# Thirty transposing loads of the expert activations begun by ScalarE instead of SyncE

## The chip, the cores and the metric

The kernel runs on one core of one Trainium2 chip. The core has five engines, each with an instruction stream of its own: TensorE (PE, matrix products), VectorE (DVE), ScalarE (ACT), GpSimd (POOL) and SyncE (SP, which only begins transfers here). They meet through semaphores: an instruction may wait until a counter has reached a value, and may raise one when it is done. Transfers are begun by SP, ACT or POOL and carried out by 16 shared DMA engines. The metric is the device time of one execution in microseconds; less is better.

## The reference

One decoder block of a first kind is followed by one of a second kind, for 256 tokens of width 2048 in float32. The change lies in the last part of the first block, a layer of 16384 experts of which each token uses 8 x 16:

```python
def peer_ffn(h, w_pq, peer_keys, peer_u, peer_v):
    ...                                   # for each token: idx and gate of 8 heads x 16 experts
    def one_block(args):
        x_blk, i_blk, g_blk = args
        u = jnp.take(peer_u, i_blk, axis=0)
        a = jax.nn.gelu(jnp.einsum("td,thkd->thk", x_blk, u)) * g_blk
        v = jnp.take(peer_v, i_blk, axis=0)
        return jnp.einsum("thk,thkd->td", a, v)
```

The kernel doesn't gather. It multiplies all tokens with all 16384 rows of `peer_u`, applies gelu, multiplies with a dense table of gates that is zero where a token doesn't use an expert, and multiplies the result with all rows of `peer_v`. Beside that it already computes the second block's modulation, `mod = jax.nn.silu(c) @ w_mod[l] + b_mod[l]`, on VectorE.

## The kernel before

**Tiles of weights.** All weights stream through the core as 512 KB tiles (128 partitions x 1024 values). For each tile SP begins a load into one of 8 buffers `raw` (`load`, L445); ACT copies it, rounded, into one of 4 buffers `hi` (`split`, L795 to L802); DVE forms the remainder `lo` = `raw` - `hi` (L1521); PE then runs 12 products of 512 columns on `hi` and `lo` (`tile`, L2657 to L2683). ACT may write the `hi` buffer of tile t+4 when PE has finished tile t, and SP may load tile t+8 when DVE has finished with tile t.

**The expert stage.** The 16384 experts are 32 blocks of 512. A block has 8 tiles of `peer_u` ("up") and 8 of `peer_v` ("down"). After a block's 8 up tiles ACT applies gelu in PSUM and copies the result as 16-bit halves to `Ab` (`gelu`, L1079 to L1088, two instructions of each); POOL stores `Ab` to a scratch in memory (`a_store`, L679). A transposing load brings the scratch back with experts on partitions, into one of two buffers `AT` (`act_in`, L530 to L535; 32 of them). DVE multiplies `AT` with the gates into `P32` (`gate`, L1988 to L1996), ACT rounds that to `Ph` (`act_high`, L1140 to L1144), DVE forms the remainder `Pl` (`low`, L2001), and `Ph` and `Pl` enter the 8 down tiles. The down tiles form four chunks c = 0 to 3 of two tiles each, in two pairs of PSUM banks in turn; when a chunk is complete, DVE adds it to `X` (`v_add`, L2023 to L2029; `pair_add`, L2066 to L2071). PE must not begin chunk 2 before chunk 0 is added, since both use the same banks.

**Order of the blocks.** The up tiles of the first 24 blocks come first (`AHEAD`). Then come 8 main blocks (`MAIN`; L1161 on ACT, L2031 on DVE): 8 up tiles of block 24+v, then 8 down tiles of block v. Their 16 tiles are called tile 0 to 15 here; tile 8 begins the down part, and chunk 0 is tiles 8 and 9, chunk 2 is tiles 12 and 13. Then come 11 pairs of blocks (`act_pair`, L1186, and `dve_pair`, L2073) of 16 down tiles for two blocks in the order of `PAIR`, and a last pair.

**What stands in each queue.** ACT and DVE work through lists written out in the source. In a main block ACT has: splits, with a load of `w_mod` (1 MB, `mod_load`, L1156) after every second one; gelu after the split of tile 11; splits of tiles 12 and 13; `act_high`; further splits. DVE has: splits, with a product of a `w_mod` row (2.28 us, L2020) after every second one; split of tile 12; `gate` of the next block; split of tile 13; `v_add` of chunk 0; `low`; further splits. SP's queue holds the loads of the weights, and `act_in` of the block two further on between the 8 up tiles and the 8 down tiles, or, in a pair, twice between down tiles.

Of the kernel before, what the change touches and what calls it, by code (L numbers as in the profile page):

```python
# [12 lines left out]
U16 = mybir.dt.uint16  # L13
# [7 lines left out]
D, KD = 2048, 16  # L21
# [19 lines left out]
MAIN = NBLK - AHEAD  # L41
# [129 lines left out]
def build(nc, A, out):  # L171
    V, SC, PE_, GP = nc.vector, nc.scalar, nc.tensor, nc.gpsimd
    ctx = ExitStack()
    with ctx:
# [102 lines left out]
        AT = at("AT", [P, 2, JB, S], W0 + 20)  # L277
# [166 lines left out]
        def _(sp):  # L444
# [83 lines left out]
                    load(tile("peer_v", b * (4 * TL) + j), n + j, off)  # L528

            def act_in(v, q):  # L530
                if not isinstance(v, int) or v >= 2:
                    sp.wait_ge(gated, v * 2 - 2)
                sp.wait_ge(a_st, v * 16 + 64)
                block = adram[v] if isinstance(v, int) else adram[bass.ds(v, 1)].rearrange("b s a n -> (b s) a n")
                sp.dma_start_transpose(AT[:, q].bitcast(U16), block.rearrange("s a n -> (s a) n")).then_inc(a_in[q], 16)  # L535

            up(0, n0)
            queries_in(2)
# [6 lines left out]
            with sp.Fori(0, MAIN // 2) as it:  # L545
                for q in range(2):
                    up(it * 2 + (AHEAD + q), n0 + AHEAD * TC + 16 * q, it * 32)
                    act_in(it * 2 + (q + 2), q)
                    down(it * 2 + q, n0 + AHEAD * TC + 16 * q + 8, it * 32)
            with sp.Fori(0, AHEAD // 2 - 1) as b:  # L550
                for i, (e, c) in enumerate(PAIR):
                    if i in (5, 7):
                        act_in(b * 2 + (MAIN + 2 + i // 7), i // 7)
                    for j in range(TL):
                        load(tile("peer_v", b * (8 * TL) + ((MAIN + e) * 4 * TL + c * TL + j)),
                             n0 + AHEAD * TC + 16 * MAIN + TL * i + j, b * 16)
# [235 lines left out]
        def _(act):  # L792
            st = Steps(act, act_step)

            def split(n0, off=0):  # L795
                if n0 >= TOTAL:
                    return
                act.wait_ge(raw_ready[n0 % RAW], 16 * (n0 // RAW + 1) + off * (16 // RAW))
                if n0 >= SPL:
                    act.wait_ge(tile_used, n0 - SPL + 1 + off)  # L800
                w = TW // 2 if n0 in ROPE_TILES else TW
                SC.copy(hi[:, n0 % SPL, 0:w], raw[:, n0 % RAW, 0:w]).then_inc(hi_ready, 1)  # L802
# [276 lines left out]
            def gelu(b, n, bank=0):  # L1079
                act.wait_ge(tile_used, n)  # L1080
                for t in range(TT):
                    SC.activation(ps[:, bank + t], ps[:, bank + t], ACT.Gelu_apprx_tanh,
                                  scale=stat[:, ROOT2 + 2 + t:ROOT2 + 3 + t]).then_inc(scaled, 1)
                if not isinstance(b, int) or b:
                    act.wait_ge(a_st, b * 16 + 48)
                for t in range(TT):
                    act.wait_ge(scaled, b * 2 + (t + 7))
                    SC.copy(Ab[:, t], ps[:, bank + t].bitcast(U16).rearrange("p (n a) -> p a n", a=2)).then_inc(a_ok, 1)  # L1088
# [51 lines left out]
            def act_high(v, q, used):  # L1140
                act.wait_ge(gated, v * 2 + 2)
                if used is not None:
                    act.wait_ge(tile_used, used)
                SC.copy(Ph[:, q], P32[:, q]).then_inc(ph_ok, 1)  # L1144
# [9 lines left out]
            n0 = BASE["peer"] + AHEAD * TC  # L1154

            def mod_load(u, rr):  # L1156
                act.dma_start(mraw[:, u % 4], A["w_mod"][bass.ds(rr * KD + u, 1)].rearrange("a p n -> p (a n)")
                              ).then_inc(mod_in[u % 4], 16)

            act.wait_ge(g_st[1], 32)  # L1160
            with act.Fori(0, MAIN // 4) as rr:  # L1161
                act.wait_ge(mod_used, rr * KD)
                for u in range(2):
                    mod_load(u, rr)
                for i in range(4):
                    n, off = n0 + 16 * i, rr * 64
                    for j in range(4):
                        split(n + 4 + 2 * j, off)
                        split(n + 5 + 2 * j, off)
                        u = 4 * i + j  # L1170
                        if u + 2 < KD:
                            act.wait_ge(mod_used, rr * KD + u)
                            mod_load(u + 2, rr)
                    gelu(rr * 4 + (AHEAD + i), off + (n + 8))
                    split(n + 12, off)
                    split(n + 13, off)
                    act_high(rr * 4 + (i + 1), (i + 1) % 2, off + n)
                    for j in range(14, 20):
                        split(n + j, off)
# [6 lines left out]
            def act_pair(v, n, u):  # L1186

                for p in range(16):
                    if p == 13:
                        act_high(v + 2, 0, n + 14)  # L1190
                    split(n + SPL + p)
                    if p == 0:
                        act_high(v + 1, 1, n)
                    elif p in (4, 6, 10, 12):
                        mod_fetch(u + 2 + (4, 6, 10, 12).index(p))

# [2314 lines left out]
```

## Time and profile before

| | us |
|---|---|
| median of 3 runs (lowest to highest) | 3500.81 (3499.68 to 3501.33) |
| the profiled execution | 3499.71 |
| its span in the profile | 3498.1 |
| PE busy | 3483.0 |
| DVE busy | 2642.4 |
| ACT busy | 1904.9 |

The span runs from the first to the last instruction. An engine is busy while it executes; issuing a transfer doesn't count, but the timeline shows it with a "q" behind the engine's name (ACTq, SPq), and the duration there is the time that the engine's instruction stream spent on the issue. Of the 3498.1 us the main blocks take 1283 to 1631 us, and the pairs 1631 to about 2110 us. A tile takes PE 2.72 us in both. Adjacent instructions of an engine overlap by about 0.1 us in the timeline, so a duration is a little more than the step to the next start.

### The profile page before, as it was taken

The numbers are of one execution on the slowest core, as the hardware profiler recorded it, in microseconds if no ns is written. First come the engines' busy times: TensorE is split into PE (matmuls) and PEld (weight loads), VectorE is DVE, ScalarE is ACT, GpSimd is POOL, SyncE is SP. The second block draws the span as 40 slices with busy tenths as digits, with TensorE's granted clock in tenths as the row PEclk, the third lists the DMA queues.
The fourth block names the chain that finished last, engine by engine and source line by source line (L and its number), as shares of the span: only waits on it lengthen the run. The fifth ranks groups of instructions, "written<-read, shape, count | busy, mean of one in ns | idle before, by whom it ended". The sixth has DMA issues, their size and how long they took to land.

```text
span 3498.1 us, 47372 instructions
## 1 busy us (share of the span) xinstructions
PE 3483.0 (100%) x16532; PEld 2906.2 (83%) x16532; DVE 2642.4 (76%) x3553; ACT 1904.9 (54%) x2469; POOL 150.9 (4%) x207
## 2 busy tenths in 40 slices
PE   9999999999999999999999999999999999999999
PEld 7898888888888888888888888878888888888887
DVE  6654557679888878888888888899976666666668
ACT  6554444555588864444444446557754555545544
POOL 2100000000000000000000001010000000000000
PEclk9999999999999999999999999999999999999999
DMA  8556658876667799999999997655556577877774
GB/s 279 184 159 199 195 175 286 301 231 216 218 217 262 258 321 360 318 334 327 338 338 339 338 338 242 180 178 171 167 176 222 176 222 213 233 230 213 233 228 145
DMA packets 319649, 853.39 MB, mean 244 GB/s; under 512 B 134209, under 2 KB 134849, under 8 KB 305137
## 3 DMA queue, kind: packets, MB, share of 16 engines
q1 hardware_dynamic: 250352, 660.69, 59.6%
q10 hardware_dynamic: 52560, 112.28, 9.3%
q0 software_dynamic: 16560, 78.08, 6.3%
q8 instruction: 110, 1.80, 0.2%
q14 instruction: 67, 0.54, 0.0%
HBM read 773.72 MB, written 49.31 MB: 235 GB/s over the span
## 4 chain that ended last, share of the span: by engine, by line
PE 97%; DVE 1%; ACT 1%; DMA 1%; issue 1%; SPq 0%; POOL 0%; ACTq 0%; DVEq 0%
PE ps L2681 29%; PE ps L2682 29%; PE ps L2683 29%; PE ps L3311 2%; PE ps L2774 1%; PE ps L2775 1%; PE ps L2776 1%; PE ps L3027 1%; PE ps L3315 1%; PE ps L2789 1%; PE ps L3153 0%; DMA mraw<-in_w_mod 0%; PE ps L2724 0%; ACT hi L802 0%; DVE lo L1521 0%
## 5 line engine op out<-in xcount | busy, mean ns | idle before, releaser
L1521 DVE TENSOR_TENSOR lo<-raw,hi 128x1024 fp32r<-128x1024 f32 (+1 forms) x1213 | 1468.2, 1218 | 769.5 <-ACT hi L802 767.8
L802 ACT CAST hi<-raw 128x1024 fp32r<-128x1024 f32 (+1 forms) x1215 | 1270.8, 1048 | 1428.2 <-PE ps L2683 1313.6
L2681 PE MATMUL ps<-hi,xx 128*128 128x512 f32 x2752 | 1083.1, 394 | 1.2 <-DVE lo L1516 0.6
L2682 PE MATMUL ps<-lo,xx 128*128 128x512 f32 x2752 | 1072.2, 390 | 0.0
L2683 PE MATMUL ps<-hi,xx 128*128 128x512 f32 x2752 | 1071.6, 389 | 0.0
L2681 PEld LDWEIGHTS ps<-hi,xx 128*128 128x128 f32 x2752 | 517.0, 188 | 110.9 <-issue 5.5
L2683 PEld LDWEIGHTS ps<-hi,xx 128*128 128x128 f32 x2752 | 516.7, 188 | 109.2
L2682 PEld LDWEIGHTS ps<-lo,xx 128*128 128x128 f32 x2752 | 517.3, 188 | 102.8
L2681 PE MATMUL ps<-hi,Ph 128*128 128x512 f32 x1020 | 397.4, 390 | 0.4 <-DVE X L2029 0.4
L2683 PE MATMUL ps<-hi,Pl 128*128 128x512 f32 x1020 | 396.9, 389 | 0.0
L2682 PE MATMUL ps<-lo,Ph 128*128 128x512 f32 x1020 | 396.8, 389 | 0.0
L2681 PEld LDWEIGHTS ps<-hi,Ph 128*128 128x128 f32 x1020 | 191.4, 188 | 40.4 <-DVE X L2029 0.8
L2683 PEld LDWEIGHTS ps<-hi,Pl 128*128 128x128 f32 x1020 | 191.4, 188 | 39.8
L2682 PEld LDWEIGHTS ps<-lo,Ph 128*128 128x128 f32 x1020 | 191.5, 188 | 39.6
L2681 PE MATMUL ps<-hi,Fh 128*128 128x512 f32 x348 | 135.6, 390 | 0.8 <-DVE Fl L2558 0.7
L2682 PE MATMUL ps<-lo,Fh 128*128 128x512 f32 x348 | 135.4, 389 | 0.0
L2683 PE MATMUL ps<-hi,Fl 128*128 128x512 f32 x348 | 135.4, 389 | 0.0
L2060 DVE SCALAR_TENSOR_TENSOR mraw<-mraw,cS 128x2048 f32<-128x2048 f32 x48 | 109.6, 2283 | 0.0
L1094 ACT ACTIVATE oh<-oh,selR 128x128 fp32r<-128x128 f32 x256 | 82.1, 397 | 13.1 <-DVE oh L1964 13.1
L2537 DVE SCALAR_TENSOR_TENSOR cv<-UP,ccol,cv 128x255 f32<-128x255 f32 (+1 forms) x176 | 73.2, 478 | 8.5 <-ACT cv L1422 7.7
L2681 PEld LDWEIGHTS ps<-hi,Fh 128*128 128x128 f32 x348 | 65.3, 188 | 15.1 <-DVE Fl L2558 1.1
L2020 DVE SCALAR_TENSOR_TENSOR mraw<-mraw,cS 128x2048 f32<-128x2048 f32 x32 | 73.1, 2285 | 5.4 <-DMA mraw<-in_w_mod 5.3
(515 smaller groups left out, 3783.2 us busy)
## 6 DMA issues: line engine op xcount, KB each, us to landing
raw<-in_peer_u SPq DMA_DIRECT2D x256, 512.0 KB, 4.4
raw<-in_peer_v SPq DMA_DIRECT2D x256, 512.0 KB, 6.6
mraw<-in_w_mod ACTq DMA_DIRECT2D x96, 1024.0 KB, 7.8
raw<-in_w_up SPq DMA_DIRECT2D x176, 512.0 KB, 4.2
raw<-in_w_in SPq DMA_DIRECT2D x143, 512.0 KB, 3.6
raw<-in_in SPq DMA_DIRECT2D x128, 512.0 KB, 3.6
raw<-in_w_down SPq DMA_DIRECT2D x88, 512.0 KB, 4.5
raw<-in_out SPq DMA_DIRECT2D x64, 512.0 KB, 4.0
```

The costliest lines, as they stand in the source:

```text
L802: SC.copy(hi[:, n0 % SPL, 0:w], raw[:, n0 % RAW, 0:w]).then_inc(hi_ready, 1)
L1094: low = SC.activation(oh2[:, g % 2, k, 1], oh2[:, g % 2, k, 0].bitcast(F32), ACT.Copy, scale=selR[:, t:t + 1])
L1521: V.tensor_tensor(lo[:, n0 % SPL, 0:w], raw[:, n0 % RAW, 0:w], hi[:, n0 % SPL, 0:w].bitcast(F32), ALU.subtract).then_inc(lo_ready, 1)
L2020: V.scalar_tensor_tensor(mraw[:, u % 4], mraw[:, u % 4], 1.0, cS[:], ALU.mult, ALU.mult, accum_out=mcol[:, bass.ds(rr, 1), u]).then_inc(mo ...
L2060: V.scalar_tensor_tensor(row, row, 1.0, cS[:], ALU.mult, ALU.mult, accum_out=mcol[:, part, u % KD:u % KD + 1]).then_inc(mod_used, 1)
L2537: ins = V.scalar_tensor_tensor(dst, src, ccol[:, q + 1 - tap:q + 2 - tap], dst, ALU.mult, ALU.add)
L2681: PE_.matmul(acc, xhi[:, k0 + k, xs], H, start=s0, stop=False)
L2682: PE_.matmul(acc, xhi[:, k0 + k, xs], L, start=False, stop=False)
L2683: mm = PE_.matmul(acc, xlo[:, k0 + k, xs], H, start=False, stop=s1)
L2774: PE_.matmul(acc, H, xhi[:, k0 + k], start=first and k == 0 and f % 2 == 0, stop=False)
L2775: PE_.matmul(acc, H, xlo[:, k0 + k], start=False, stop=False)
L3311: PE_.matmul(both, H, xx[:, :, k0 + k], start=first and k == 0, stop=False)
```

## The change

Of the 32 transposing loads, SP keeps the first two. The other 30 are taken out of SP's queue and written into ACT's list: in a main block right behind the gelu, ahead of the splits of tiles 12 and 13; in a pair behind the splits of p = 2 and p = 8. They wait for the same two semaphores as before: `gated` (the buffer's last user is done) and `a_st` (the scratch is stored). So that the block number is a constant, ACT's loop over 2 x 4 main blocks is written out.

```diff
             def act_in(v, q):
-                if not isinstance(v, int) or v >= 2:
-                    sp.wait_ge(gated, v * 2 - 2)
                 sp.wait_ge(a_st, v * 16 + 64)
-                block = adram[v] if isinstance(v, int) else adram[bass.ds(v, 1)].rearrange("b s a n -> (b s) a n")
-                sp.dma_start_transpose(AT[:, q].bitcast(U16), block.rearrange("s a n -> (s a) n")).then_inc(a_in[q], 16)
+                sp.dma_start_transpose(AT[:, q].bitcast(U16), adram[v].rearrange("s a n -> (s a) n")).then_inc(a_in[q], 16)
...
                     up(it * 2 + (AHEAD + q), n0 + AHEAD * TC + 16 * q, it * 32)
-                    act_in(it * 2 + (q + 2), q)
                     down(it * 2 + q, n0 + AHEAD * TC + 16 * q + 8, it * 32)
             with sp.Fori(0, AHEAD // 2 - 1) as b:
                 for i, (e, c) in enumerate(PAIR):
-                    if i in (5, 7):
-                        act_in(b * 2 + (MAIN + 2 + i // 7), i // 7)
...
             def mod_load(u, rr):
-                act.dma_start(mraw[:, u % 4], A["w_mod"][bass.ds(rr * KD + u, 1)].rearrange("a p n -> p (a n)")
-                              ).then_inc(mod_in[u % 4], 16)
+                act.dma_start(mraw[:, u % 4], A["w_mod"][rr * KD + u]).then_inc(mod_in[u % 4], 16)
+
+            def act_in(v, q):
+                act.wait_ge(gated, v * 2 - 2)
+                act.wait_ge(a_st, v * 16 + 64)
+                act.dma_start_transpose(AT[:, q].bitcast(U16), adram[v].rearrange("s a n -> (s a) n")).then_inc(a_in[q], 16)
 
             act.wait_ge(g_st[1], 32)
-            with act.Fori(0, MAIN // 4) as rr:
+            for rr in range(MAIN // 4):
                 act.wait_ge(mod_used, rr * KD)
                 for u in range(2):
                     mod_load(u, rr)
                 for i in range(4):
-                    n, off = n0 + 16 * i, rr * 64
+                    n, off = n0 + 16 * i + 64 * rr, 0
...
                     gelu(rr * 4 + (AHEAD + i), off + (n + 8))
+                    act_in(rr * 4 + (i + 2), i % 2)
                     split(n + 12, off)
                     split(n + 13, off)
                     act_high(rr * 4 + (i + 1), (i + 1) % 2, off + n)
...
                     if p == 0:
                         act_high(v + 1, 1, n)
+                    elif p in (2, 8):
+                        act_in(v + 2 + p // 8, p // 8)
                     elif p in (4, 6, 10, 12):
                         mod_fetch(u + 2 + (4, 6, 10, 12).index(p))
```

ACT's program in a main block, from the `w_mod` load ahead of the gelu to the split of tile 13, before (CAST is the split, COPY the copy to `Ab`, ISA and REGISTER_ALU compute and wait in registers):

```order
L1157 DMA mraw<-in_w_mod 128x2048
L1082 ACTIVATE ps<-ps,stat 128x512 x2
L1085 ISA
L1087 ISA
L1088 COPY Ab<-ps 128x1024
L1087 REGISTER_ALU
L1088 COPY Ab<-ps 128x1024
L800 REGISTER_ALU
L802 CAST hi<-raw 128x1024
L800 REGISTER_ALU
L802 CAST hi<-raw 128x1024
```

and the same place now:

```order
L1151 DMA mraw<-in_w_mod 128x2048
L1076 ACTIVATE ps<-ps,stat 128x512 x2
L1082 COPY Ab<-ps 128x1024 x2
L1156 DMA_TRANSPOSE AT<-act_scratch 128x4x512
L796 CAST hi<-raw 128x1024 x2
```

The transposing load stands between the second copy and the split of tile 12, and behind the `w_mod` load in ACT's own transfers; the register instructions are gone.

ACT's program in the first pair, from its first split to the second `Ph`, before:

```order
L802 CAST hi<-raw 128x1024
L1144 CAST Ph<-P_122 128x1024
L802 CAST hi<-raw 128x1024 x4
L1184 DMA mraw<-in_w_mod 128x2048
L802 CAST hi<-raw 128x1024 x2
L1184 DMA mraw<-in_w_mod 128x2048
L802 CAST hi<-raw 128x1024 x4
L1184 DMA mraw<-in_w_mod 128x2048
L802 CAST hi<-raw 128x1024 x2
L1184 DMA mraw<-in_w_mod 128x2048
L1144 CAST Ph<-P_122 128x1024
```

and now:

```order
L796 CAST hi<-raw 128x1024
L1138 CAST Ph<-P_122 128x1024
L796 CAST hi<-raw 128x1024 x2
L1156 DMA_TRANSPOSE AT<-act_scratch 128x4x512
L796 CAST hi<-raw 128x1024 x2
L1183 DMA mraw<-in_w_mod 128x2048
L796 CAST hi<-raw 128x1024 x2
L1183 DMA mraw<-in_w_mod 128x2048
L796 CAST hi<-raw 128x1024 x2
L1156 DMA_TRANSPOSE AT<-act_scratch 128x4x512
L796 CAST hi<-raw 128x1024 x2
L1183 DMA mraw<-in_w_mod 128x2048
```

The two transposing loads stand behind the third and the ninth split; the `w_mod` loads keep their places.

SP's queue where the up tiles of a main block end and the down tiles begin, before:

```order
L448 DMA raw<-in_peer_u 128x1024
L532 ISA
L533 ISA
L535 ISA
L535 DMA_TRANSPOSE AT<-act_scratch 128x4x512
L447 REGISTER_ALU
L448 ISA
L448 DMA raw<-in_peer_v 128x1024
```

and now:

```order
L448 DMA raw<-in_peer_u 128x1024
L447 REGISTER_ALU
L448 ISA
L448 DMA raw<-in_peer_v 128x1024
L447 REGISTER_ALU
```

SP goes from the last up tile to the first down tile with no other transfer between.

## Rows read from the trace of the kernel before

**Rows 1.** The page, busy time of each engine (share of the span), instructions.

```profile
PE 3483.0 (100%) x16532; PEld 2906.2 (83%) x16532; DVE 2642.4 (76%) x3553; ACT 1904.9 (54%) x2469; POOL 150.9 (4%) x207
```

**Rows 2.** Waits of PE, whole run: engine, line, releaser: us, times, longest.

```profile
PE ps L2732 <- DMA const<-in_const: 4.4, 1, 4.4
...
PE ps L2681 <- DVE X L2029: 0.4, 1, 0.4
```

**Rows 3.** Transposing loads into AT: issue ns min/median/max, first and last.

```profile
L535 SPq DMA_TRANSPOSE AT<-act_scratch x32: 3110/5190/9112, 1228.2 to 2073.9; - x32
```

**Rows 4.** Transposing loads of the second block's FFN, begun by ACT.

```profile
L1404 ACTq DMA_TRANSPOSE UP<-act_scratch x18: 3158/4048/5339, 2849.8 to 3393.8; - x18
```

**Rows 5.** Timeline of ACT around one of these: start, us, instruction [idle before].

```profile
2936.81 4.54 ACTq L1404 DMA_TRANSPOSE UP<-act_scratch  x1
2941.45 2.00 ACT L802 CAST hi<-raw 128x1024 fp32r<-128x1024 f32 x2 [3.67 <-issue]
```

**Rows 6.** Timeline of ACT in main block 1, gelu to split of tile 12.

```profile
1347.12 0.34 ACTq L1157 DMA_DIRECT2D mraw<-in_w_mod  x1
...
1349.08 1.93 ACT L1088 COPY Ab<-ps 128x1024 uint16<-128x1024 uint16 x2
1350.88 1.08 ACT L802 CAST hi<-raw 128x1024 fp32r<-128x1024 f32 x1
```

**Rows 7.** Timeline of DVE, main block 1: remainder of tile 12, add of chunk 0.

```profile
1351.99 1.23 DVE L1521 TENSOR_TENSOR lo<-raw,hi 128x1024 fp32r<-128x1024 f32 x1 [0.49 <-ACT hi L802]
...
1355.47 1.28 DVE L2029 TENSOR_TENSOR X<-X,ps 128x512 f32<-128x512 f32 x2
```

**Rows 8.** Timeline of PE, first product of tile 12 in main blocks 0 and 1.

```profile
1314.00 0.50 PE L2681 MATMUL ps<-hi,Ph 128*128 128x512 f32 x1 [0.39 <-DVE X L2029]
...
1357.65 0.39 PE L2681 MATMUL ps<-hi,Ph 128*128 128x512 f32 x1
```

**Rows 9.** SP at 1318 us: weight load, its landing, transposing load right behind it.

```profile
L448 SPq DMA_DIRECT2D raw<-in_peer_u x1: 333/333/333, 1318.2 to 1318.2; - x1
...
DMA to landing us min/median/max: 9.6/9.6/9.6
...
L535 SPq DMA_TRANSPOSE AT<-act_scratch x1: 8708/8708/8708, 1318.9 to 1318.9; - x1
```

**Rows 10.** Landing of the w_mod load ahead of gelu, main blocks 0, 1, 2, 4, 6.

```profile
DMA to landing us min/median/max: 10.4/10.4/10.4
...
DMA to landing us min/median/max: 8.0/8.0/8.0
...
DMA to landing us min/median/max: 7.0/7.0/7.0
...
DMA to landing us min/median/max: 8.6/8.6/8.6
...
DMA to landing us min/median/max: 6.4/6.4/6.4
```

**Rows 11.** Timeline of ACT in main block 0, w_mod load and splits behind gelu.

```profile
1304.72 0.34 ACTq L1157 DMA_DIRECT2D mraw<-in_w_mod  x1
...
1308.07 2.02 ACT L802 CAST hi<-raw 128x1024 fp32r<-128x1024 f32 x2
```

**Rows 12.** Timeline of the second pair: ACT's split p = 2, DVE, and PE's tile 8.

```profile
1681.59 1.05 ACT L802 CAST hi<-raw 128x1024 fp32r<-128x1024 f32 x1 [1.43 <-PE ps L2683]
...
1686.96 2.28 DVE L2060 SCALAR_TENSOR_TENSOR mraw<-mraw,cS 128x2048 f32<-128x2048 f32 x1
...
1691.97 1.28 DVE L2071 TENSOR_TENSOR X<-X,ps 128x512 f32<-128x512 f32 x2
...
1694.93 0.39 PE L2681 MATMUL ps<-hi,Ph 128*128 128x512 f32 x1
```

**Rows 13.** Timeline of PE, the product at which the start's slow ones end.

```profile
7.96 0.40 PE L2683 MATMUL ps<-hi,xx 128*128 128x512 f32 x1
```

**Rows 14.** Windows, run's end: us, busy of PE, PEld, DVE, ACT, POOL, PEclk, DMA.

```profile
3494.00:3498.10 4.10, 0.10 (x1) 0.00 (x0) 1.52 (x3) 0.00 (x0) 0.00 (x0) 0.79 0.34 128
```

## The prediction

> **What bounds the kernel now.** I read the page's busy times first, then PE's waits, then the issue times of the transposing loads, then the timelines of ACT, DVE and PE at the two places where the loads go. PE is busy for 3483.0 of 3498.1 us [rows 1], and its longest wait, 4.4 us, is at the very start; in the expert stage it waits once, 0.4 us for an add to `X` [rows 2]. So nothing in that stage can be won beyond 0.4 us. The question is only what ACT, DVE and PE lose when ACT begins the loads. SP, which begins them now, has nothing else to do in that time than run ahead.
>
> **What the issue costs an engine.** A transposing load holds SP for 3.1 to 9.1 us, 5.2 in the middle [rows 3]. The same instruction exists on ACT in the second block's FFN: 18 loads, 3.2 to 5.3 us, median 4.05 [rows 4]. There ACT stands still through it: the issue begins at 2936.81, takes 4.54, and the next split begins at 2941.45, 0.10 us after its end, with 3.67 us of idle time put down to the issue [rows 5]. PE loses nothing in the FFN, since no other work of ACT crowds that place. So the removed part (30 issues off SP) is worth nothing, or the 0.4 us at most, and the added part (30 issues on ACT) holds the splits behind it.
>
> The Trainium skill says otherwise: "DMA: Bandwidth & Descriptors", section "Issuing engines are not separate DMA queues", holds that the time of an engine to begin a transfer is usually small against the transfer. The trace disagrees for this form, with an issue of 4.05 us where a plain load of 1 MB takes 0.34 [rows 4, 6]; by the page's rule the change would be worth nothing, which is one of the rivals below.
>
> **How long the issue is in a main block.** The longest issues on SP are longer for a reason: a weight load begun at 1318.2 lands 9.6 us later, at 1327.8, and the transposing load right behind it in the same queue begins at 1318.9, takes 8.7 and so ends at 1327.6 [rows 9]. The issue ends 0.2 us before the load in front of it has landed. On ACT the load in front is the 1 MB of `w_mod` begun just before the gelu. So I take the end of the issue as the later of two times: start plus 4.05, or landing of the `w_mod` load less 0.25.
>
> In block 1 that load begins at 1347.12 and lands after 8.0 us [rows 6, 10], at 1355.1; the issue ends at 1354.9, and the split of tile 12 begins at 1354.95 instead of 1350.88 [rows 6]: 4.1 us late. As a formula: late = landing - 3.9. The landings of 7.0 and 8.6 us in blocks 2 and 4 [rows 10] give 3.1 and 4.7. Block 0 is crowded: the load begins at 1304.72, lands after 10.4, and the split stands at 1308.07 [rows 10, 11], so 10.4 - 0.15 - 3.35 = 6.9. In block 6 the landing is 6.4 [rows 10], and 6.4 - 3.9 = 2.5 is about what the issue's own 4.05 gives; block 5 has nearly the same, and blocks 3 and 7 have no `w_mod` load left in front. Own time: the stream of ACT may begin the issue when the second copy to `Ab` is handed over, which I put at 1349.3, 0.2 after the first copy begins [rows 6]; 1349.3 + 4.05 + 0.10 - 1350.88 = 2.57. If the issue waits for the second copy to begin, it starts at 1350.1 and these four blocks are 0.8 later each.
>
> **What of it reaches PE.** A late split alone would hide, because `lo` of tile 12 is done at 1353.2 [rows 7] and PE begins the tile at 1357.65 [rows 8], 4.4 us later. But tile 12 opens chunk 2, which must wait for the add of chunk 0, and that add stands behind `lo` of tile 12, the gate product and `lo` of tile 13 in DVE's list. It ends at 1355.47 + 1.28 = 1356.75 [rows 7]. PE follows such an add by 0.06 us, so it has 1357.65 - 0.06 - 1356.75 = 0.84 us to spare. DVE waits for ACT at that very `lo` (0.49 us idle, ACT hi) [rows 7], so every microsecond by which the split is late passes to the add, and all beyond 0.84 passes to PE. In block 0 nothing is to spare: PE already waits there for this add [rows 8].
>
> PE's loss is then 6.9 in block 0, 4.1 - 0.84 = 3.3 in block 1, 2.3 in block 2, 3.9 in block 4, and 1.7 in each of 3, 5, 6 and 7: together 23.2 us. PE makes up nothing afterwards, as it is the bound of every stage.
>
> **The pairs.** The load behind p = 2 (tile 3 is the next split) has its cover. The split begins at 1681.59 in the second pair; the issue starts 0.08 later, and with an issue of D the next split begins at 1681.77 + D. Behind it stand on DVE, in steps, `lo` 1.1 after the split begins, 1.14 for itself, 2.21 for a `w_mod` row, twice 1.14 for `lo`, and 1.28 for the add: the add of chunk 0 ends at 1689.8 + D, against PE's tile 8 at 1694.93 [rows 12]. So D up to 5.1 is free, and no `w_mod` load is in flight in front. With 4.05 the 11 loads cost nothing; with SP's 5.2 they cost 0.1 each; with 6.5, 1.4 each. The load behind p = 8 has no such add close behind it; by the same steps it is free up to about 7. I take zero for both, 15 us as the upper end. Should a `w_mod` load land late behind them, DVE waits; it has about 10 us from issue to use there, and I count nothing.
>
> **PE's clock.** In the last 4.1 us, with PE at rest, the granted clock averages 0.79 of 2.4 GHz [rows 14], so it fell to 1.2 within that time. At the start PE begins at 4.4 [rows 2] and its products come at full pace from about 7.96 [rows 13]: 3.5 us at half pace, a loss of 1.8 us. A stall of some microseconds may bring that loss again. I count it for the two longest stalls, 2 x 1.8 = 3.6; the bounds are none and all eight, 0 and 14. The Trainium skill, "TensorE: Matmul & The Clock Gate", section "HAM oscillation — how this bites in real kernels", says that gaps of PE in a loop bring the lower clock back each time; by it the upper end would be nearer. No row shows a gap of 2 to 7 us inside this run.
>
> **Sum.** 23.2 + 0 + 3.6 = 26.8 us on the profiled execution's 3499.7 (span 3498.1 and 1.6 around it), so 3526.5. The runs' median of 3500.8 stands 1.1 above that execution, so 3528. The lower bound: every issue at 4.05 from its own start gives 7 x 1.7 + 2.6 = 14.5, or 3515; at 3.2, the shortest on ACT [rows 4], about 8. The upper: 23 + 14 + 10 = 47, or 3548.
>
> **Rivals.** (a) The issue doesn't lengthen behind the `w_mod` load, as that load has few and large pieces: all main blocks at 1.7, no clock loss, 3511 to 3517. For it speaks the FFN [rows 4, 5], against it SP [rows 9]. (b) The pairs lose too, since the DMA engines are busier there than in the FFN and issues of 5.5 to 6.5 pass the 5.1 of cover: another 5 to 15, about 3540. SP's own times speak for it [rows 3], the missing load in front against it. (c) The clock falls in nearly every main block: about 3539. (d) Not slower: the issue is begun while ACT still executes the gelu's two copies and ends soon after them. Copies and spare together give 1350.88 - 1349.3 + 0.84 - 0.1 = 2.3 us; from an issue below that nothing reaches PE, and the wait of 0.4 us goes if SP is freed: 3500.4. Against it: none of 50 issues is below 3.1 [rows 3, 4]. This is also what the page's rule on issuing would give.
>
> **How the numbers follow.** Forecast 0.55, (a) 0.15, (b) 0.12, (c) 0.11, (d) 0.05, else 0.02. A measurement of this kernel can tell about 0.2%, 7 us. The forecast, (a), (b) and (c) lie beyond it; the rest, with issues near 3.1, doesn't. Slower 0.93, same 0.05, faster 0.02. The range of 8 in 10 is 3511 to 3548, from (a) to the upper bound.
>
> **What would show it.** Right: PE's waits gain a row "ps <- DVE X" of the main blocks' add with about 8 entries of 1.5 to 7 us, the longest in block 0; ACT's splits of tile 12 are idle before with "issue"; the transposing loads of ACT take 4 to 8.5 us in the main blocks and about 4 in the pairs; the time between pairs stays 43.5 us. Wrong: issues of 3 us, tiles 12 that start on time, or waits in the pairs as long as in the main blocks.

## The result, and the profile after

The changed kernel takes 3554.44 us (median of 4 runs, 3548.41 to 3567.25) against 3500.95 for the kernel before (4 runs): the ratio is 1.0154, with an interval from 1.0136 to 1.0172. It is slower, as predicted, but by 53.5 us instead of 27, and outside the range. Its profiled execution has a span of 3554.6 us, 56.5 more than that of before.

PE's busy time, on the page, answers to [rows 1]. It has risen by 17.4 us with the same number of instructions, so some products have become longer:

```profile
PE 3500.4 (98%) x16532; PEld 2915.7 (82%) x16532; DVE 2639.7 (74%) x3553; ACT 1900.8 (53%) x2469; POOL 151.0 (4%) x207
```

PE's waits (line, releaser: us, times, longest) show the other part. The first line, the add to `X` of the main blocks, had 0.4 us, once [rows 2]; the other two, the add of the pairs and a remainder, are the pairs' share:

```profile
PE ps L2682 <- DVE X L2030: 37.7, 8, 9.2
...
PE ps L2682 <- DVE X L2072: 1.3, 2, 0.7
PE ps L2682 <- DVE lo L1522: 1.3, 3, 0.5
```

The transposing loads, now on ACT (issue in ns, least, median and greatest, and time to landing), answer to [rows 3] and [rows 4]; the longest is nearly three times the FFN's median:

```profile
L1156 ACTq DMA_TRANSPOSE AT<-act_scratch x30: 3586/4883/11725, 1305.1 to 2145.8; - x30
...
DMA to landing us min/median/max: 5.6/9.3/20.4
```

Main block 1 shows the whole chain. The timeline of ACT (start, us, instruction, idle time before it), to compare with [rows 6]: the issue holds ACT for 8.46 us, and the split of tile 12 begins 0.09 us after its end.

```profile
1358.36 0.33 ACTq L1151 DMA_DIRECT2D mraw<-in_w_mod  x1
...
1360.62 8.46 ACTq L1156 DMA_TRANSPOSE AT<-act_scratch  x1
...
1369.17 1.99 ACT L796 CAST hi<-raw 128x1024 fp32r<-128x1024 f32 x2 [6.80 <-PE ps L2684]
```

(The idle time is put down to a product that PE had finished long before; the row above it tells the cause.) The timeline of DVE, to compare with [rows 7]: `lo` of tile 12, which waited 0.49 us for ACT before, waits 7.39, and the add comes as much later.

```profile
1370.25 1.22 DVE L1522 TENSOR_TENSOR lo<-raw,hi 128x1024 fp32r<-128x1024 f32 x1 [7.39 <-ACT hi L796]
...
1373.73 1.28 DVE L2030 TENSOR_TENSOR X<-X,ps 128x512 f32<-128x512 f32 x2
```

The timeline of PE, to compare with [rows 8]: tile 12 begins 0.05 us after the add, and its first nine products are 0.43 us apart.

```profile
1375.06 0.79 PE L2682 MATMUL ps<-hi,Ph 128*128 128x512 f32 x1 [5.94 <-DVE X L2030]
1375.65 0.63 PE L2683 MATMUL ps<-lo,Ph 128*128 128x512 f32 x1
...
1379.42 0.40 PE L2683 MATMUL ps<-lo,Ph 128*128 128x512 f32 x1
1379.65 0.40 PE L2684 MATMUL ps<-hi,Pl 128*128 128x512 f32 x1
```

The windows of the same stretch (busy of PE, PEld, DVE, ACT, POOL, then the granted clock, DMA share, GB/s): during the stall the clock falls from 2.4 GHz to 1.2, stays there for the 4 us in which the products are slow, and comes back.

```profile
1369.00:1371.00 2.00, 0.12 (x1) 0.00 (x0) 0.75 (x1) 1.83 (x2) 0.00 (x0) 1.00 1.38 52
...
1373.00:1375.00 2.00, 0.00 (x0) 0.00 (x0) 2.00 (x4) 2.00 (x3) 0.00 (x0) 0.50 1.05 408
1375.00:1379.00 4.00, 3.94 (x9) 3.13 (x10) 4.00 (x6) 0.65 (x1) 0.00 (x0) 0.50 0.91 290
1379.00:1383.00 4.00, 4.00 (x18) 3.26 (x17) 1.83 (x3) 1.16 (x2) 0.00 (x0) 0.96 0.67 246
```

The eight main blocks, read from the timelines (stall: the step from the start of tile 11 to that of tile 12, less the usual 2.72; slow: the step from tile 12 to 13, less 2.72):

| block | 0 | 1 | 2 | 3 | 4 | 5 | 6 | 7 | sum |
|---|---|---|---|---|---|---|---|---|---|
| issue, us | 11.72 | 8.46 | 5.89 | 4.26 | 8.51 | 9.00 | 6.15 | 3.85 | 57.8 |
| stall | 9.37 | 6.10 | 3.54 | 1.91 | 6.15 | 6.64 | 3.79 | 1.50 | 39.0 |
| slow | 2.56 | 2.11 | 1.44 | 0.13 | 2.51 | 1.84 | 2.57 | 0.17 | 13.3 |

The stall is the issue less 2.35 to 2.37 us in every block. From their first down tile to the first pair, the main blocks take 52.0 us more than before (there, block 0 alone had 0.7 us of stall and slow products), and the pairs take 4.1 more: 56.1 of the 56.5 us by which the span grew.

### The profile page after: what moved, and what is told of

The parts are those of the page before. It is cut to its first block, busy times and chain, and to the rows that moved or that the text cites. A ratio compares the mean times of both kernels' runs of the same rounds, so it can differ in the third digit from the quotient of the medians.

```text
span 3554.6 us, 47198 instructions
## 1 busy us (share of the span) xinstructions
PE 3500.4 (98%) x16532; PEld 2915.7 (82%) x16532; DVE 2639.7 (74%) x3553; ACT 1900.8 (53%) x2469; POOL 151.0 (4%) x207
## 4 chain that ended last, share of the span: by engine, by line
PE 93%; DVE 2%; issue 2%; ACT 1%; ACTq 1%; DMA 0%; SPq 0%; DVEq 0%; POOL 0%
PE ps L2682 28%; PE ps L2683 28%; PE ps L2684 28%; PE ps L3312 2%; PE ps L2775 1%; PE ps L2777 1%; PE ps L2776 1%; ACTq L1156 1%; PE ps L3028 1%; PE ps L3316 1%; DVE lo L1522 1%; ACT hi L796 1%; PE ps L2790 1%; PE ps L3154 0%; PE ps L2725 0%
## 5 line engine op out<-in xcount | busy, mean ns | idle before, releaser
L2682 PEld LDWEIGHTS ps<-hi,Ph 128*128 128x128 f32 x1020 | 194.8, 191 | 86.5 <-DVE X L2030 41.1
L2061 DVE SCALAR_TENSOR_TENSOR mraw<-mraw,cS 128x2048 f32<-128x2048 f32 x48 | 109.7, 2285 | 0.4 <-DMA mraw<-in_w_mod 0.4
L2684 PEld LDWEIGHTS ps<-hi,Fl 128*128 128x128 f32 x348 | 65.3, 188 | 13.6
```

The source lines that it names most:

```text
L2061: V.scalar_tensor_tensor(row, row, 1.0, cS[:], ALU.mult, ALU.mult, accum_out=mcol[:, part, u % KD:u % KD + 1]).then_inc(mod_used, 1)
L2682: PE_.matmul(acc, xhi[:, k0 + k, xs], H, start=s0, stop=False)
L2684: mm = PE_.matmul(acc, xlo[:, k0 + k, xs], H, start=False, stop=s1)
```

## The experiments

Theory: the issue holds ACT; what it holds longer than a fixed cover reaches PE one to one, through the add behind the split; the longer stalls bring the lower clock. Rivals: the transfers, not the hold, do it; the slow products have another cause; the pairs take part. Each time below stands beside 3499.4 to 3500.9 us of the kernel before in the same comparison, and 3554.4 of the changed one.

### The main blocks alone, the pairs alone

Of the changed kernel, the first keeps only the main blocks' loads on ACT, the second only the pairs'; the others are SP's, where they stood before. Ahead of the first pair, the engine that takes the loads over waits until the other's last load has landed.

```diff
# x1_main: pairs on SP again
+            sp.wait_ge(a_in[1], 96)            # ahead of the first pair
...
-                    elif p in (2, 8):
-                        act_in(v + 2 + p // 8, p // 8)
# x2_pairs: main blocks on SP again
                     gelu(rr * 4 + (AHEAD + i), off + (n + 8))
-                    act_in(rr * 4 + (i + 2), i % 2)
...
+            act.wait_ge(a_in[1], 96)           # ahead of the first pair
```

> Only the 8 loads of the main blocks are begun by ScalarE; the 22 of the pairs are back in SyncE's queue. By the changed kernel's trace, where PE waits 37.7 us for the add in 8 places, the main blocks carry nearly all of the loss: about 52 of 56 us, so 3551 to 3554. Rival: the loss is spread over all 30 loads (busier DMA engines, ScalarE late everywhere): about a third of it, near 3520.

> Only the 22 loads of the pairs are begun by ScalarE, the 8 of the main blocks by SyncE as before. With a cover of 5.1 us behind p = 2 and issues of 3.6 to 6.0 us: 3501 to 3505, a loss of 0 to 4 us, and part of the 4 us seen there should go, since the first pair's long issue came after a crowded main stage. Rival (loss spread over all 30): near 3535.

x2_pairs: 3506.0 us, ratio 1.0012 (1.0003 to 1.0022), just above what was expected: the pairs cost about 5 us. x1_main: 3571.0, ratio 1.0188 (1.016 to 1.0216), more than the whole change. Its main blocks lose what they lose in the changed kernel (stalls 38.0, slow 11.9). The rest is lost in its pairs (56 us in its profiled execution, with 3605 us the slowest of four), by SP's loads, whose median issue went from 5.2 us [rows 3] to 11. The timeline of SP, in the kernel before and in x1_main (a row "x12" is twelve loads in a row):

```profile
1645.84 26.10 SPq L448 DMA_DIRECT2D raw<-in_peer_v  x12
```

```profile
1746.86 17.17 SPq L535 DMA_TRANSPOSE AT<-act_scratch  x1
1764.30 19.42 SPq L448 DMA_DIRECT2D raw<-in_peer_v  x12
1784.06 10.01 SPq L535 DMA_TRANSPOSE AT<-act_scratch  x1
```

SP, late by one long issue, sends twelve weight loads at 1.6 us each, where it took 2.2 before, and the next transposing load queues up behind them. This explains how the state keeps itself up. Its start points to the edit itself: at the added wait SP stands still once, for 14.6 us, until ACT's last load lands at 1664.7; then it sends six weight loads in 3.3 us, and its first transposing load behind them takes 14.2 (waits of SP):

```profile
SPq L550 <- DMA AT<-act_scratch: 14.6, 1, 14.6
```

A kernel with similar stalls, all loads on SP and no such wait (x7_hold below) had none of it. So what x1_main loses in its pairs tells nothing of the change. The two runs agree that the main blocks lose about 50 us and the pairs about 5.

### A hold without a transfer

The kernel before, all its loads on SP, with copies of a PSUM bank on ACT in place of the issue, 0.6 us each.

```diff
                     gelu(rr * 4 + (AHEAD + i), ...)
+                    for k in range((2, 5, 8, 12)[i]):
+                        SC.copy(ps[:, 3], ps[:, 2]).then_inc(scaled, 1)
+                        act.wait_ge(scaled, ...)
                     split(n + 12, off)
```

> The kernel before, its transposing loads all in SP's queue, with ACT held behind the gelu of the main blocks by 2, 5, 8 and 12 copies of a PSUM bank (0.6 to 0.75 us each with the wait between them) in blocks 0, 1, 2, 3 and again in 4, 5, 6, 7. Theory: what costs is that ACT doesn't split in that time, whatever it does; the stalls of PE ahead of tile 12 are the hold less 0.84 us (block 0: the hold), so about 1.4, 2.6, 4.7, 7.5, 0.5, 2.6, 4.7 and 7.5, and the clock adds some 2 us behind those above 2 to 3: 3540 to 3548. Rival: the loss comes from the transfers (the load in ACT's queue, or the weights that it delays); then a hold without a transfer costs a small part of this, under 3515.

3540.03 us, ratio 1.0113 (1.0097 to 1.013). The timelines of ACT (the hold of block 3) and of PE (its tile 12):

```profile
1449.74 7.24 ACT L1176 COPY ps<-ps 128x512 f32<-128x512 f32 x12
```

```profile
1462.97 0.79 PE L2684 MATMUL ps<-hi,Ph 128*128 128x512 f32 x1 [6.30 <-DVE X L2032]
1463.56 0.63 PE L2685 MATMUL ps<-lo,Ph 128*128 128x512 f32 x1
```

Holds of 1.22, 3.02, 4.83 and 7.24 us gave stalls of 0.45, 2.26, 4.06 and 6.46 in blocks 4 to 7: the hold less 0.77 each time, against 0.84 predicted from [rows 7, 8]. Stalls of 27.7 and slow steps of 12.4 make up the 40.1 by which the span grew. No transfer is needed; the hold alone does it.

### The add ahead of the late split

In the changed kernel, DVE's add of chunk 0, and then that of chunk 1 too, is put ahead of the remainders that wait for ACT.

```diff
+                    v_add(v, 0, off + (n + 10))
                     split(n + 12, off)
                     gate(v + 1, ...)
                     split(n + 13, off)
-                    v_add(v, 0, off + (n + 10))
+                    v_add(v, 1, off + (n + 12))        # x13_adds_first only
                     low(v + 1, (i + 1) % 2)
```

> The changed kernel, with DVE's add of chunk 0 in the main blocks put ahead of the remainder of tile 12 instead of behind that of tile 13; ACT's list is as changed. Theory: the late split of tile 12 costs so much because the add that PE waits for stands behind it in DVE's list; then the wait for the add goes, and PE waits only for the remainder of tile 12 itself, which has about 3.6 us more cover: the stalls of 9.4, 6.1, 3.5, 1.9, 6.2, 6.6, 3.8 and 1.5 fall to about 5.8, 2.5, 0, 0, 2.6, 3.0, 0.2 and 0, 14 in all, with some 2 us of lower clock behind three or four of them; 3520 to 3526. Rival: PE waits for the late split itself or for late weights, whatever the place of the add; then 3545 or more.

> The changed kernel, with DVE's adds of chunk 0 and chunk 1 in the main blocks put ahead of the remainders of tiles 12 and 14 (with the add of chunk 0 alone moved, PE waited for the add of chunk 1 instead, 1.2 to 1.5 us in seven blocks). Theory: that second wait goes too, about 10 us of the 28 that were left; 3513 to 3522. Rival: the late splits of tiles 14 and 15 keep PE waiting at the same place for the remainders, so that nothing is won: 3526 to 3531.

x6_add_first: 3529.14, ratio 1.0081 (1.0064 to 1.0097), 25 us won, 3 less than expected. With an issue of 7.51 in block 4, tile 12 waits 1.55, and for `lo` instead of the add; issues up to 5.8 cost nothing there. But PE now waits at tile 14, for the add of chunk 1 (waits and timelines of x6_add_first):

```profile
PE ps L2682 <- DVE lo L1522: 11.6, 5, 6.6
PE ps L2682 <- DVE X L2030: 7.5, 6, 1.3
```

```profile
1492.48 7.51 ACTq L1156 DMA_TRANSPOSE AT<-act_scratch  x1
```

```profile
1502.54 0.47 PE L2682 MATMUL ps<-hi,Ph 128*128 128x512 f32 x1 [1.55 <-DVE lo L1522]
```

x13_adds_first: 3523.92, ratio 1.0061 (1.0044 to 1.0078), a little above what was expected; the waits at tile 14 are gone, and the issues in its profile happened to be longer (8.43 in block 4, stall 2.63, again the issue less 5.8). So it was the place of the add that left only 2.4 us of cover, as the prediction had it.

### What the clock takes

In the changed kernel, PE fills most of its stall with small transposes into a free bank.

```diff
                 for c in range(4):
+                    if c == 2:
+                        keep_busy((60, 40, 20, 6, 40, 44, 22, 6)[v], 2)
                     if c >= 2 or not isinstance(v, int) or v:
                         pe.wait_ge(v_out, v * 8 + (2 * c - 2))
```

> The changed kernel, and PE fills most of its stall ahead of chunk 2 in the main blocks with transposes of 128 x 128 into a free bank (60, 40, 20, 6, 40, 44, 22 and 6 of them in blocks 0 to 7, sized below the stalls of the changed kernel at about 0.12 us each). Theory: of the 54 us, 39 are the stalls themselves and 13 are products at the lower clock behind them; then the stalls stay at about 39, the step from tile 12 to tile 13 falls back from 4.2 to 5.3 us to 2.8 in all blocks, and the time is 3540 to 3544. Rival: the slow products behind a stall come from late operands or from something else than the clock; then the step stays at 4.2 to 5.3 and the time at 3550 or more.

3546.85 us, ratio 1.0127 (1.011 to 1.0144), 3 us above what was expected; the stalls stay (38.5), the slow steps fall from 13.3 to 3.8. Block 1 (timeline of PE): the stall is filled for 4.53 us, and the first product of tile 12 takes 0.50 instead of 0.79.

```profile
1368.41 4.53 PE L2733 MATMUL ps<-const 128*128 128x128 f32 x40
...
1373.63 0.50 PE L2682 MATMUL ps<-hi,Ph 128*128 128x512 f32 x1 [0.69 <-DVE X L2030]
```

The granted clock there stays at 2.4 GHz, where the changed kernel had 1.2 behind its stall (windows of x5_busy):

```profile
1373.00:1377.00 4.00, 3.37 (x15) 2.82 (x16) 4.00 (x5) 1.50 (x3) 0.00 (x0) 1.00 0.99 354
```

The two blocks that stayed slow, 0 and 2, are those in which the stall went on for some 2.8 and 3.4 us behind the last transpose (stalls of 9.6 and 5.6, less 60 and 20 transposes at 4.53 / 40 us). So the slow products are the clock's. The gain of 7.6 us is 2 less than the slow steps say; the pairs, which lost 14.3 us in its profiled execution against 4.1, may be the rest.

### What makes the issue long

Four ways to change what stands in front of the transposing load in ACT's queue. x3_wmod_behind puts the fourth `w_mod` load of a main block behind it; x8_small cuts that load to an eighth, and x10_all_small nearly all of the main blocks' `w_mod` loads; x12_mod_sp and x14_mod_sp_paced let SP begin the fourth one, the first behind the block's down tiles, the second behind the second up tile that follows; x15_two_in_front puts the third load directly in front of the fourth.

```diff
# x3_wmod_behind, x12_mod_sp, x14_mod_sp_paced
-                        if u + 2 < KD:
+                        if u + 2 < KD and j < 3:
# x3_wmod_behind
                     act_in(rr * 4 + (i + 2), i % 2)
+                    if i < 3:
+                        act.wait_ge(mod_used, rr * KD + 4 * i + 3)
+                        mod_load(4 * i + 5, rr)
# x8_small
-                            mod_load(u + 2, rr)
+                            mod_load(u + 2, rr, 256 if j == 3 else 2048)
# x10_all_small
+                w = 256 if rr or u > 3 else 2048
# x12_mod_sp, x14_mod_sp_paced: not on ACT, on SP
+                        sp.wait_ge(mod_used, r * KD + u - 2)
+                        sp.dma_start(mraw[:, u % 4], A["w_mod"][r * KD + u]).then_inc(mod_in[u % 4], 16)
# x15_two_in_front
-                        if u + 2 < KD:
+                        for w in {2: (), 3: (u + 1, u + 2)}.get(j, (u + 2,)):
```

> In each main block the 1 MB load of w_mod that stood just ahead of the gelu is begun right behind the transposing load instead. Theory Q (the issue is long because that load is in front of it in ScalarE's own queue): the issues of all 8 main blocks fall to the 3.9 to 4.3 us of blocks 3 and 7, PE waits about 1.9 us in each, hardly any clock loss: 3501 + 16 + 4 = about 3521. Theory S (the issue is long because GpSimd's store of Ab and load of gates start at the same time on the same DMA engines): the issues stay at 6 to 11 us and the time at 3545 or more.

> The changed kernel, with the fourth load of w_mod of each main block, the one that stands right in front of the transposing load, cut to an eighth (128 x 256 instead of 128 x 2048), so that part of the second block's modulation is computed from stale values. Theory: the issue is lengthened by the transfer that is still under way in front of it; then the issues of blocks 1, 2, 4, 5 and 6 fall from 5.9 to 9.0 us to the 3.9 to 4.3 of blocks 3 and 7, block 0 stays longer, the stalls fall to some 1.5 to 2.5 each, and the time is 3518 to 3530. Rival: the issue is long because the DMA engines are busy with the weights and the store at that moment, whatever stands in front in the queue; then the issues stay at 6 to 9 and the time above 3545.

> The changed kernel with all loads of w_mod in the main blocks but the first four of the first half cut to an eighth (128 x 256 instead of 128 x 2048), so that part of the second block's modulation is computed from stale values. Theory Q: what lengthens the issue is data still under way in ACT's own transfers; with none left the issues of all main blocks, block 0 included, fall to 3.5 to 4.6 us, their stalls to 1 to 2 us each (some 13 in all), the clock takes little behind stalls under 2 us, and the time is 3512 to 3522. Theory S: the weights of SP and the store of POOL under way at that moment lengthen it too; then issues of 5 to 6 us stay, as they stayed in three blocks with only the fourth load cut, block 0 stays above 8, and the time is 3530 or more.

> The changed kernel, with the fourth load of w_mod of blocks 0, 1, 2, 4, 5 and 6, full in size, begun by SP behind the loads of the block's down tiles instead of by ACT in front of the transposing load. The DMA engines have the same bytes to move at about the same time; only ACT's own queue is free in front. Theory Q (order within the queue): the issues fall as with the cut load, to 3.8 to 5.8 us in blocks 1, 2, 4, 5 and 6, and the time to 3535 to 3542. Theory S (the shared DMA engines): the issues stay at 6 to 9 us and the time at 3548 or more.

> The changed kernel, with the fourth load of w_mod of blocks 0, 1, 2, 4, 5 and 6, full in size, begun by SP behind the second up tile of the following block, which is within 1 us of where ACT began it; there SP needn't wait long for it, so that no bunch of weight loads follows, as one did when it stood behind the down tiles. Theory Q (what stands in front in the same queue sets the issue): the issues of blocks 1, 2, 4, 5 and 6 fall from 5.9 to 9.0 us to 4 to 5.5, stalls are the issues less 2.36, and the time is 3535 to 3544. Theory S (bytes under way on the shared DMA engines set it, whoever began them): the issues stay at 6 to 9 and the time above 3548.

> The changed kernel, with the third load of w_mod of each main block held back to stand directly in front of the fourth, so that 2 MB instead of 1 MB stand in ACT's queue right in front of the transposing load (blocks 0, 1, 2, 4, 5 and 6; blocks 3 and 7 as they are). Theory Q: the issues of blocks 1, 2, 4, 5 and 6 grow by 2 to 4 us, to 8 to 12, their stalls by the same, and the time is 3563 to 3575. Theory S: the same bytes are moved in the same stretch; the issues stay at 6 to 9 and the time at 3550 to 3558.

The issues in blocks 0 to 7, and the times with their ratios:

| | issues, us | time, us | ratio |
|---|---|---|---|
| changed kernel | 11.7 8.5 5.9 4.3 8.5 9.0 6.2 3.9 | 3554.4 | 1.0154 (1.0136 to 1.0172) |
| x3_wmod_behind | 9.3 4.1 5.4 3.5 5.4 4.4 4.7 5.5 | 3545.1 | 1.013 (1.0112 to 1.0148) |
| x8_small | 9.5 3.8 5.8 4.6 5.1 4.6 5.4 4.1 | 3539.8 | 1.0115 (1.0098 to 1.0132) |
| x10_all_small | 7.3 7.2 5.2 4.5 4.9 4.8 4.8 3.8 | 3544.6 | 1.0125 (1.0109 to 1.0142) |
| x12_mod_sp | 11.3 7.8 1.6 8.1 10.6 1.6 10.8 4.6 | 3553.0 | 1.0144 (1.0128 to 1.0161) |
| x14_mod_sp_paced | 11.4 5.5 2.3 3.6 7.0 1.5 5.7 5.2 | 3544.6 | 1.0128 (1.0111 to 1.0144) |
| x15_two_in_front | 12.6 9.0 10.8 3.8 9.7 9.8 9.5 4.2 | 3571.1 | 1.0198 (1.0181 to 1.0215) |

Two loads in front lengthen the issue of block 2 from 5.9 to 10.8 (timeline of ACT in x15_two_in_front):

```profile
1416.01 0.90 ACTq L1151 DMA_DIRECT2D mraw<-in_w_mod  x2
...
1418.29 10.78 ACTq L1156 DMA_TRANSPOSE AT<-act_scratch  x1
```

The load in front does count. In the mean over blocks 1, 2, 4, 5 and 6 the issue takes 7.6 us in the changed kernel (6.1 to 7.6 in the four other runs that have this queue in the main blocks: x1_main, x5_busy, x6_add_first and x13_adds_first), 9.7 with two loads in front, and 4.4 to 5.4 with the load moved behind, cut or moved to SP at the same pace; the times follow. One block alone tells little, since each value is of one execution: block 5 had 9.0 in the changed kernel and 5.4 in x5_busy. And in x14_mod_sp_paced the mean of 4.4 comes from two issues under 2.3; the other three took 5.5 to 7.0. But it is not the whole. With nothing large in front, issues of 5 us and more stay, and the own time isn't a constant of 4. x12_mod_sp came out as its Theory S says. SP, held by its wait for the buffer of `w_mod` (43.6 us in six places), sends its loads in bunches (timeline of SP in block 4, where ACT's issue begins at 1507.20):

```profile
1504.03 0.33 SPq L548 DMA_DIRECT2D mraw<-in_w_mod  x1
1504.40 3.26 SPq L448 DMA_DIRECT2D raw<-in_peer_u  x4
```

By the packet records of the traces (start and size of every packet), SP's queue moved 2.5 MB during that issue, against 1.1 MB in block 4 of the changed kernel. So bytes on the shared DMA engines seem to have taken the place of those in the queue; but blocks 2 and 5 had the same bunch and issues of 1.6 us (last section).

x3_wmod_behind, x8_small and x10_all_small took 10 to 24 us more than expected. In the first the `w_mod` issue, now behind the transposing load, itself takes 1.11 us of ACT ahead of the split instead of 0.34:

```profile
1358.25 4.06 ACTq L1156 DMA_TRANSPOSE AT<-act_scratch  x1
...
1362.35 1.11 ACTq L1151 DMA_DIRECT2D mraw<-in_w_mod  x1
1363.56 2.00 ACT L796 CAST hi<-raw 128x1024 fp32r<-128x1024 f32 x2 [3.56 <-issue]
```

In all three I had the clock wrong: stalls of 2.1 to 3 us still cost 1.5 to 1.7 us each, one of them 2.6, so shorter issues save little of that term (10.9 to 13.4 us of slow steps, against 13.3).

### A place with more cover

x4_later puts the main blocks' loads behind the split of tile 17, with the pairs as changed. x11_covered does that too and puts the first load of a pair behind p = 5 instead of p = 2.

```diff
-                    act_in(rr * 4 + (i + 2), i % 2)
...
                     for j in range(14, 20):
                         split(n + j, off)
+                        if j == 17:
+                            act_in(rr * 4 + (i + 2), i % 2)
...
-                    elif p in (2, 8):
+                    elif p in (5, 8):                  # x11_covered only
```

> The transposing load of a main block is begun by ScalarE four tiles later, behind the split of tile 17 (tile 1 of the next block), where no add to X stands close behind in VectorE's list. If the loss is the add of chunk 0 waiting for ScalarE's split, the waits of the main blocks go and only the pairs' 4 us stay: 3502 to 3506. If the loss comes from the load on ScalarE's queue as such (slower transfers, PE's products slower), it stays above 3530.

> The changed kernel with the transposing loads at places of ACT's list with more cover: in the main blocks behind the split of tile 17, in the pairs behind the split of p = 5 instead of p = 2 (where the add that follows is already behind DVE) and behind p = 8 as now. Theory: an issue of up to about 8 us costs nothing at either place, PE never waits, and the time is that of the kernel before, 3499 to 3502. Rival: the pairs' loads now stand behind a w_mod load in ACT's queue, get longer than 8 us and pass their cover: 3506 to 3525.

x4_later: 3512.96 (3501.39 to 3522.29), ratio 1.0036 (1.0021 to 1.005), 7 us above what was expected; in its profile, which has the best of these times, the stalls of the main blocks are gone. x11_covered: 3558.83, ratio 1.0171 (1.0153 to 1.0189): a plain miss. Its main blocks lose nothing either; its pairs lose 50 us, because the second load now stands 8.2 us behind the first, with a `w_mod` load between (timeline of ACT, first pair):

```profile
1654.29 6.34 ACTq L1156 DMA_TRANSPOSE AT<-act_scratch  x1
...
1660.75 0.51 ACTq L1184 DMA_DIRECT2D mraw<-in_w_mod  x1
...
1662.45 14.73 ACTq L1156 DMA_TRANSPOSE AT<-act_scratch  x1
...
1677.28 1.04 ACT L796 CAST hi<-raw 128x1024 fp32r<-128x1024 f32 x1 [13.59 <-issue]
```

More cover for one load took away the distance that kept the other short. No version tried here is faster than the kernel before; x4_later is the nearest, and what spreads its runs over 20 us stays open.

## Why the prediction was wrong in size

**What bounds the kernel, and the direction: right.** PE had nothing to win and lost what ACT held back.

**The hold and its path: right, to 0.1 us.** The prediction's chain (late split, `lo`, add, chunk 2) is the one that the changed kernel shows, x7_hold shows it without any transfer, and x6_add_first and x13_adds_first show that the add's place is the link. The cover worked out in it was 2.57 - 0.84 from an issue of 4.05, so 2.32; measured 2.36. The spare was put at 0.84; x7_hold measured 0.77.

**The length of the issue: the step that failed.** "I take the end of the issue as the later of two times: start plus 4.05, or landing of the `w_mod` load less 0.25." In blocks 3 and 7, with no load in front, 4.26 and 3.85 came out as the first half says. In the others the issue ended 1.4 to 4.8 us after the landing in front (block 1: begun at 1358.36, landed 8.6 later at 1367.0, issue ended at 1369.1):

```profile
DMA to landing us min/median/max: 8.6/8.6/8.6
```

The rule rested on one row of another queue [rows 9]. There it was no accident: by the landings in the trace, all 32 issues on SP in the kernel before ended 0.08 to 0.33 us ahead of the landing in front of them. What failed was to carry it over to ACT's queue and a load of 1 MB instead of 512 KB. The rule gave 41.0 us for the eight issues (8.4, 5.6, 4.6, 6.2 and four of 4.05), and with the landings of the changed kernel itself it gives 41.1; they took 57.8. The stalls became 39.0, 0.5 of it there before, instead of 23.2: about 15 of the 30 us that were missed.

What ends an issue on ACT instead stays open. It isn't the landing in front alone: by the packet records, the load's first packet in block 1 moved 3.9 us after the issue's start, 2.4 us before that landing. Nor is it a fixed part of the load's own 2048 packets: over all 390 issues on ACT in these runs, half ended when 484 to 562 of them had begun to move, but the eight of the main blocks at 332 to 693, and 27 at under 200, four of the long ones of x15_two_in_front among them.

**The clock: second mis-sized term.** Six of eight stalls brought the lower clock, not two, at 1.4 to 2.6 us each: 13.3 instead of 3.6. The price taken from the start of the run [rows 13] came out near (2.2 in the mean, against 1.8), but by luck in part: the granted clock of those first slow products is 1.00, so no row shows that they were the clock's (windows of the kernel before):

```profile
4.00:8.00 4.00, 3.56 (x15) 3.29 (x16) 2.08 (x4) 1.99 (x4) 0.00 (x0) 1.00 0.96 320
```

The count was an unfounded choice between bounds that the prediction had itself put at 0 and 14. What the Trainium skill says there ("TensorE: Matmul & The Clock Gate", "HAM oscillation — how this bites in real kernels"), that gaps in a loop bring the lower clock back each time, is what the trace shows here for six of the eight.

**The pairs: the rule right, the zero wrong.** "D up to 5.1 is free": in the changed kernel the two first loads of a pair that took 6.0 us cost 0.82 and 0.83, and in x5_busy one of 7.3 cost 2.22. But some issues passed the bound, and the pairs lost 4.1 us. This is rival (b), just below its price of 5 to 15. Rival (c) was right as well; (a) and (d) fell, (d) with an issue never under 3.5 in the changed kernel.

**The range** summed upper bounds of 23, 14 and 10, the last below the 15 that the prediction had named for the pairs, and had no upper bound for the one term that was a rule from another queue. Had the longest issue seen on SP, 9.1 [rows 3], been taken as an upper end in six blocks, it would have reached 6 x (9.1 - 2.3) + 2 x 1.7 + 14 + 15 = 73 us, or 3574.

## What to carry to other kernels

An engine that computes should begin a transposing load only where everything queued behind the issue has several microseconds of slack, counted through the other engines' lists and not only to the next instruction; here an add two instructions further on DVE set the price. The length of such an issue isn't its own: look at what stands in front of it in the same queue, and on the engines, and don't carry a rule from one queue to another: here it held in 32 rows of 32 on SP, and in none of the six main blocks with a load in front on ACT. And a stall of PE is to be priced with the slow products behind it: behind stalls of 2 to 4 us those cost 1.4 to 2.6 us here, with two exceptions.

## What the runs showed of the hardware that was not expected

- **Short stalls were cheap, longer ones not.** Over the main blocks of the runs above, 14 stalls between 0.4 and 1.94 us cost 0.10 to 0.17 us of slow products; of those of 2.1 us and more that PE didn't fill, all but two cost 1.4 to 2.6. The two, of 2.63 and 3.71 us, cost 0.12 and 0.17. Stalls of 9 us cost no more than those of 4.
- **An issue can be much shorter.** In x12_mod_sp and x14_mod_sp_paced, blocks 2 and 5 had issues of 1.5 to 2.3 us, ended before any packet of the load had moved, and cost PE nothing (timeline of ACT in x14_mod_sp_paced, block 5):

```profile
1546.78 1.51 ACTq L1160 DMA_TRANSPOSE AT<-act_scratch  x1
...
1548.41 1.08 ACT L800 CAST hi<-raw 128x1024 fp32r<-128x1024 f32 x1
```

  Why the queue took those whole stays open. They show that the 4 us are not the work of beginning the load; that they are a wait for room in the queue is argued, not shown. A fifth short issue is of another kind: in block 7 of x1_main SP stood still at its added wait, none of its loads was under way, and ACT's issue took 2.06 us and the load landed 4.4 us after its start (timeline of ACT):

```profile
1660.28 2.06 ACTq L1162 DMA_TRANSPOSE AT<-act_scratch  x1
```

  By this one row, about half of the 4 us that the prediction took for the load's own time comes with the other transfers. The Trainium skill's sentence that the time to begin a transfer is usually small against the transfer ("DMA: Bandwidth & Descriptors", "Issuing engines are not separate DMA queues") holds for the first four, with 1.5 to 2.3 us of 8 to 32 until the landing, and not for the rest.
- **Long issues can feed themselves**, as SP's did in x1_main: 11 us in the middle instead of 5.2, with bunches of weight loads between, in all 11 pairs behind one hold of 14.6 us.
